# One product of TensorE's expert loop moved across the loop's edge, in a two-layer decoder trunk

## The reference, cut to what matters

```python
def hierarchical_moe(x, wg, bg, we, be, w1, w3, w2):   # per layer
    ...  # top-1 of 4 groups, top-2 of its 8 experts for each of 256 tokens
    def expert_block(args):
        xb, e = args
        return (jax.nn.silu(xb @ w1[e]) * (xb @ w3[e])) @ w2[e]
    ...  # the results, times their gates, are summed for each token
```

## Time and profile before

| what | us |
|---|---|
| median of 3 runs | 1485.36 (1485.21 to 1488.62) |
| the profiled execution | 1488.3 |
| its span in the profile | 1486.5 |
| first `hidden` of layer 0's loop starts | 327.8 |
| last `results` of layer 0's loop starts | 772.4 |
| first `hidden` of layer 1's loop starts | 1008.4 |
| last `results` of layer 1's loop starts | 1467.1 |

### The profile page before, as it was taken

The page is one execution under the profiler, slowest core; times in us unless marked ns, Lnnn a source line. Parts: engine busy times, 40 slices in busy tenths (PEclk is TensorE's granted clock), DMA queues, the critical chain, the costliest instruction groups (busy, mean ns, idle before and its releaser), DMA issues.

```text
span 1486.5 us, 32857 instructions
## 1 busy us (share of the span) xinstructions
PE 1188.6 (80%) x11743; PEld 734.9 (49%) x11749; DVE 404.9 (27%) x1077; ACT 168.5 (11%) x469; POOL 31.0 (2%) x79
## 2 busy tenths in 40 slices
PE   8999998986878777577789999998788766666564
PEld 7884447543444434344447866654444433333332
DVE  1863631351222112112124223252222111111113
ACT  0211411110111001001011001210111000000001
POOL 3000000000000000000000000000000000000000
PEclk9999999988999889889989999989899888888887
DMA  9756115259999999999995446354799999999994
GB/s 314 271 174 223 57 56 206 107 203 383 404 430 429 428 428 429 430 427 428 429 410 222 170 165 243 129 198 171 319 426 430 429 428 429 429 429 427 429 429 168
DMA packets 64536, 473.21 MB, mean 318 GB/s; under 512 B 4156, under 2 KB 11644, under 8 KB 39916
## 3 DMA queue, kind: packets, MB, share of 16 engines
q1 hardware_dynamic: 62284, 465.78, 76.7%
q0 software_dynamic: 2208, 6.81, 1.3%
HBM read 471.52 MB, written 1.05 MB: 318 GB/s over the span
## 4 chain that ended last, share of the span: by engine, by line
PE 55%; DMA 35%; issue 5%; DVE 3%; ACT 1%; SPq 0%; DVEq 0%; POOL 0%; POOLq 0%
DMA ring<-in_moe_w_dram 35%; PE bank L526 14%; PE bank L904 14%; PE bank L539 7%; PE bank L920 3%; PE bank L928 2%; PE bank L890 2%; PE bank L706 2%; PE bank L499 1%; PE bank L661 1%; PE bank L863 1%; PE bank L850 1%; PE bank L826 1%; PE bank L911 1%; PE bank L694 1%
## 5 line engine op out<-in xcount | busy, mean ns | idle before, releaser
L904 PE MATMUL bank<-ring,xT 128*32 128x256 f32 x4672 | 359.0, 475 | 245.2 <-DMA ring<-in_moe_w_dram 177.3
L904 PEld LDWEIGHTS bank<-ring,xT 128*32 128x32 f32 x4672 | 195.8, 135 | 409.0 <-issue 309.9
L526 PE MATMUL bank<-xT,ring 128*128 128x256 f32 x832 | 184.3, 384 | 6.1 <-DVE xT L1012 4.8
L526 PEld LDWEIGHTS bank<-xT,ring 128*128 128x128 f32 x832 | 159.7, 193 | 30.1 <-issue 8.0
L1405 DVE SCALAR_TENSOR_TENSOR xT<-xT,bank 64x256 f32<-64x256 f32 x73 | 30.3, 415 | 405.8 <-ACT xT L1624 405.8
L920 PE MATMUL bank<-slot,xT 128*32 128x256 f32 x2336 | 139.5, 379 | 0.6 <-DVE xT L1415 0.3
L539 PE MATMUL bank<-ring,slot 128*128 128x512 f32 x256 | 111.5, 593 | 4.0 <-ACT slot L1602 2.0
L920 PEld LDWEIGHTS bank<-slot,xT 128*32 128x32 f32 x2336 | 77.9, 109 | 49.8 <-issue 4.3
L1624 ACT ACTIVATE xT<-bank 64x256 f32<-64x256 f32 x73 | 27.5, 377 | 590.8 <-PE bank L904 590.8
L1391 DVE TENSOR_TENSOR xT<-iota,place 128x64 f32 (+1 forms) x73 | 16.5, 226 | 276.9 <-issue 274.3
L928 PE MATMUL bank<-xT 32*128 32x256 f32 x1200 | 85.9, 400 | 5.0 <-issue 5.0
(11 more groups left out here) (254 smaller groups left out, 779.1 us busy)
## 6 DMA issues: line engine op xcount, KB each, us to landing
ring<-in_moe_w_dram SPq DMA_DIRECT2D x128, 2048.0 KB, 32.4
slot<-in_moe_w_dram SPq DMA_DIRECT2D x64, 2048.0 KB, 37.9
ring<-in_od_w_in_dram SPq DMA_DIRECT2D x6, 2048.0 KB, 20.0
ring<-in_xa_wq_dram SPq DMA_DIRECT2D x4, 2048.0 KB, 11.5
ring<-in_xa_wo_dram SPq DMA_DIRECT2D x4, 2048.0 KB, 10.9
ring<-in_ev_w_in_dram SPq DMA_DIRECT2D x3, 2048.0 KB, 14.7
ring<-in_mem_wk_dram SPq DMA_DIRECT2D x2, 2048.0 KB, 15.5
ring<-in_mem_wv_dram SPq DMA_DIRECT2D x2, 2048.0 KB, 10.6
```

The source lines that it names most:

```text
L526: ins = mm(ps, w[:, k, c0:c0 + P], rhs[:, k, :], start=(k == 4), stop=(k == 3))
L904: ins = mm(b1[qs[2 * m + h], 0:S], xg[:, k, :], ws[m][:, k, h, :, :], start=(k == 0), stop=(k == KC - 1))
```

## The change

TensorE's `unit` is split into `head` (the waits for tokens and `w1`/`w3`, and `hidden`) and `rest` (all else). The first unit's `head` stands before the loop and before the wait for `units`. In the loop each body begins with `load_units` for its own expert and for the next, does `rest`, then the nest (`head` and `rest` of the further units), and ends with the `head` of the next expert, behind an `If` in two of the three bodies. The order of TensorE's matmuls stays the same. `units` gets one more zero column, which GpSimd clears at the start.

```diff
-        units = sb("units", [1, DEPTH, 2, NE + 1], I32)
+        units = sb("units", [1, DEPTH, 2, NE + 2], I32)
...
-                pe.wait_ge(units_ready, L + 1)
-
-                def unit(s, ready, n):
+                def head(s, ready, n):
 
                     pe.wait_ge(fam.gathered, n)
                     pe.wait_ge(loaded[s[0]], ready[0])
                     pe.wait_ge(loaded[s[1]], ready[1])
                     hidden(fam, s, xgT)
+
+                def rest(s, ready, n):
+
                     pe.wait_ge(fam.y_ready, n)
                     scatter(fam, comb, y)
...
+                def due(s, i):
+
+                    return [(i + (moe_base[L][s[k]] + 1)) * 16 for k in range(3)]
+
+                head(moe_slots[L][0], due(moe_slots[L][0], 0), 1)
+                pe.wait_ge(units_ready, L + 1)
+
                 with nc.Fori(0, TURNS, engines=[pe.engine], head_slot={pe.engine: 0}) as i:
                     for j in range(SETS):
                         m, first = load_units(pe, L, i * SETS + j)
-                        s_ = moe_slots[L][j]
-                        ready = [(i + (moe_base[L][s_[k]] + 1)) * 16 for k in range(3)]
+                        m_next, first_next = load_units(pe, L, i * SETS + j + 1)
+                        s_, s_next = moe_slots[L][j], moe_slots[L][(j + 1) % SETS]
                         if j < NE % SETS:
-                            unit(s_, ready, first + 1)
+                            rest(s_, due(s_, i), first + 1)
                         else:
                             with pe.If(m > 0):
-                                unit(s_, ready, first + 1)
+                                rest(s_, due(s_, i), first + 1)
                             pe.nop()
...
-                                                    unit(s_, ready, first + ra * 4 + rb * 2 + rc + 2)
+                                                    head(s_, due(s_, i), first + ra * 4 + rb * 2 + rc + 2)
+                                                    rest(s_, due(s_, i), first + ra * 4 + rb * 2 + rc + 2)
...
+                        following = due(s_next, i + (j + 1) // SETS)
+                        if j + 1 < NE % SETS:
+                            head(s_next, following, first_next + 1)
+                        else:
+                            with pe.If(m_next > 0):
+                                head(s_next, following, first_next + 1)
+                            pe.nop()
...
-            ms(units[:, :, :, NE:NE + 1], 0)
+            ms(units[:, :, :, NE:NE + 2], 0)
```

## The result

The changed kernel takes 1491.4 us (median of 15 runs, 1487.4 to 1494.1), the kernel before 1485.2 in the same comparison: a ratio of 1.004, with a 95% interval of 1.003 to 1.005. It is slower by about 6 us. The time lies in the forecast range of 1481 to 1495; its likeliest case, no measurable change, was not quite what happened, and the case "slower" was given 0.32. The profiled execution took 1492.5 us (span 1490.8), 4.3 us more span than before; the medians differ by some 2 us more than the two profiled executions, and that part has no row. In this execution the first `hidden` of layer 0 starts at 324.9 us instead of 327.8 and takes 3.66, both as forecast.

The account below looks back on a forecast made before the run. Weight transfers at 428 GB/s bound the kernel except near loop starts and ends. Terms of +4.85 us there and -2.15 for code waits gave +2.7, a median of 1488.1 us, no measurable change; range 1481 to 1495.

Parts of the forecast that it names:

- the four places named: In each layer, loop start until transfers never run dry, and last weights' landing to loop end; together +4.85 us.
- layer 0's anchor: Moment from which layer 0's weight transfers never run dry, 382.6 us before; forecast at 380 or a few us earlier.
- The price of the exposed loads: Between `hidden` and `scatter`: two loads, wait and branch, less the sequencer's 1.3 us lead, expose 1.55 us, 0.95 behind slow products.
- The closing sequence: After each layer's last `results`: one load more, 1.3 us, and 0.2 for branches, together +1.5 us.
- Layer 0 to the anchor: Layer 0's first turn: three transitions lose 1.75 us each, two units' exposed loads cost 1.55 each; together -2.15 us.
- waits for code: At layer 0's first-turn jumps `hidden` may partly run during instruction waits; layer 1's entry may gain one; -2.15 us for all.
- Layer 1: Start until transfers never run dry: +1.1 us, plus at most 2.7 for a possible entry wait; end: +2.45 us.
- Rival 3: Instruction waits in layer 0 gain nothing, or layer 1's entry gets one: 1490.2 to 1492.9 us, slower; chance 18%.
- Rivals 1 and 2: Queue hides the loads, exposure 0.2 us, 1478.5 us, 8%; or nothing hides them, 2.85 us everywhere, 1499.7 us, 7%.
- rival 4: Instruction waits in layer 0's first turn swallow two whole products, -7.3 us: 1482.9 us, the same; chance 10%.
- rival 5: The loop outgrows the instruction memory and each turn fetches code anew: +154 us, time 1640 us; chance 3%.

Follow-up runs that it names:

- `a_hoist`: The changed kernel with the closing sequence's `load_units` moved ahead of the loop; 1488.7 us, ratio 1.0018 to the kernel before.
- `a_late`: The changed kernel with the next expert's `load_units` moved from the body's top to behind the nest, right ahead of its `head`; 1489.5 us, ratio 1.0036.
- `carry`: The changed kernel with one `load_units` a body instead of two, the expert's own values kept in registers from the body before; 1476.7 us, ratio 0.994.
- `b_two_loads`: The kernel before with a second, unused `load_units` beside its own, between `results` and `hidden`; 1501.1 us, ratio 1.0105.

## Why the prediction was right, and where it was not

**What bounds the kernel** held: the stretches at 428 GB/s did not change, and the difference arose at the four places named, but for 1.2 us between layer 0's anchor and its last landings.

**The price of the exposed loads** was forecast as 1.55 us behind a `hidden` and 0.95 behind a slow one. Behind one at full pace it is 1.5 to 1.6 in two bodies of three, which fits a lead of 1.3 (2.85 - 1.5). In the third body it is 2.0 to 2.1: the end of the turn and the jump back now stand between `hidden` and `scatter`, which the forecast priced at nothing. Expert 30 is such a place, with 2.09 where 0.95 stood. Behind slow products the gap was anything from 0.4 to 1.6: 0.73 at expert 29, 1.16 at layer 1's expert 31, 0.59 and 0.39 in the first turn, 1.53 behind the fourth `hidden`. The gaps before `hidden` fell as forecast (0.5 to 0, 3.84 to 2.04, 3.49 to 1.90).

**The clock gave back what the gaps took.** With shorter waits in front, products ran faster: expert 30's took 3.66 us and not 6.47, `hidden` behind layer 1's nest 3.66 and not 5.00, the last one of layer 1 5.35 and not 6.35. That is some 5 us that no term of the forecast holds. At the end of layer 0 the gaps and the closing came to +3.8 where +3.45 had been forecast; less 2.8 for expert 30's product and with 0.4 for a slower one of expert 29 the end became 1.3 us longer.

**The closing sequence** was forecast at +1.5 and measured at +1.8 in each layer; `a_hoist`, `a_late` and `carry` move it by 1.3, 1.5 and 1.3 us for a load each. **The last scatter**, 2.09 instead of 1.15 us, was in no term: +0.9 in each layer, and the granted clock of 0.50 shows why.

**Layer 0 to the anchor** was forecast at -2.15 without the waits for code, and those were given -2.15 for both layers together. Measured in layer 0: -3.3. The layout by the Trainium skill (Runtime: NRT & Kernel Launch, Instruction fetch mechanics) gave 36 matmuls of expert 1 and a few of expert 2 ahead of the edge; the trace has 38 and 14. With the head at slot 96 the split is gone, which bears the page out. Together 38 + 14 matmuls, 3.0 us, ran ahead of missing code. What the forecast missed took part of it back: the first `results`, which was to stay where it was, ends 0.9 us later (338.47 for 337.58), since `gather` and `results` took 1.93 and 2.59 us, and behind the first wait `scatter` and `gather` ran at half pace (2.09 and 1.86 us from 346.40 on). Of the 3.3 us only 2.1 arrive at the landing of expert 29 (732.18 for 734.28). Where the other 1.2 went is open: by 734.2 us the changed kernel had moved some 1.3 MB more than the other by the same time (413 for 410 GB/s from 320 on), 3.0 us of the stream, so the stream kept the lead and the single load's landing did not. In layer 1 the distance from the anchor to the last landing is the same in both, 410.2 us.

**Layer 1** was forecast at +1.1 to the anchor, plus up to 2.7 for a wait at the entry. The wait came: 3.23 us of gap where 1.5 is the price of the loads, +1.7, of which 1.0 goes with another address of the loop. The anchor is 1.3 us later, because `hidden` behind the nest ran in 3.66 us and not in 5.00. The end was forecast at +2.45 and is +2.0 (1.16 of gap, 1.8 of closing, less 1.0 for the faster product), plus the slow scatter.

**The sum** was +2.7 us; the span moved by +4.3 and the median by +6.2. That it came so near is in part luck, since the misses have both signs. The starts of the two loops, waits for code included, were to give 3.2 us and gave 1.0; the two ends were to cost 5.9 and cost 3.3, thanks to the faster products; the two slow scatters, +1.9, were in no term. The mechanism, loads that TensorE's lead does not cover, is right and its price too; missing are a term for TensorE's clock, in both directions, and one for the jump back that moved in with the loads. Rival 3 (the code waits gain nothing, or layer 1's entry gets one; 1490.2 to 1492.9) had the right time; its second half came true, its first did not. Rivals 1 and 2 are ruled out by the gaps of 1.5 us, rival 4 (two whole products ahead of the missing code) by the 52 matmuls where it needed 128, rival 5 by the absence of instruction packets from that queue behind 1075 and from 380 to 780 us.

## What to carry to other kernels

Software-pipelining a loop whose trip data are loaded on the chip doubles the loads of a body unless the next body's values are kept; carry them in registers, and the same rotation turns from +0.4% to -0.6%. The sequencer's work counts by place: what stands in one row between two products of the engine is free only up to the engine's lead (here 1.3 us), and above it each further piece is paid in full, the loop's own jump back (0.5 us) included; with three loads it was paid again in clock. Look at the loop's closing as well: there nothing hides a load, and a value that does not change can be loaded ahead of the loop. It then stands at the loop's entry, and is won only if something hides it there: both kernels that moved it without `carry` paid it back at layer 1's entry.

## What the runs showed of the hardware

A gap of 1.5 us between `hidden` and `scatter` left the pace behind it as it was (`scatter` 1.15 us). Behind gaps of 2.75 us and more in one kernel most `scatter`s took 2.09 us, some 1.15, and the mean granted clock of the stretch was 0.80, for 0.91 in the changed kernel. Ahead of the last scatter, 2.5 us of idle time in the kernel before left it at 1.15; with 3.0 to 5.9 us it took 2.09 in layer 0 of all seven kernels that have such a gap, while in layer 1 it took 1.15 behind 3.0 us in `carry` and 1.64 behind 3.8 in `b_two_loads`. Gaps near 2 us show both: in the changed kernel `scatter` took 1.15 us behind one of 2.09 at 758, and 1.94 behind another of 2.09 at 1115. So the length of the gap alone does not decide, and what else does was not tested. And the address of a loop alone, with all instructions the same, moved the end of layer 0's fourth product by 3.2 us.
